# Keys, values and two retention heads move into a kernel's front, and one more conditioning job to TensorE

## What is computed

```python
c_act = silu(c)
mod = c_act @ w_ada + b_ada                 # (2048,) @ (2048, 12288)
sh1, sc1, gt1, sh2, sc2, gt2 = split(mod, 6)
h = modulate(rms_norm(x, g_mix), sh1, sc1)
proj = h @ w_in + b_in                      # 2048 x 5376
rq, rk, rv, rg, aq, ak, av = split(proj)    # 4 x 1024, 1024, 128, 128
mix = concat([retention(rq, rk, rv, rg), window_attention(aq, ak, av, sinks)]) @ w_out
x = x + gt1 * mix
h = modulate(rms_norm(x, g_ffn), sh2, sc2)
x = x + gt2 * conv_glu(h, w_up, w_conv, b_conv, w_down)    # d_ff 5632
f_shift, f_scale = split(c_act @ w_final_ada + b_final_ada, 2)
y = modulate(rms_norm(x, g_final), f_shift, f_scale)
```

## Time and profile before

| what | value |
|---|---|
| median of 3 runs | 1285.28 us (1285.04 to 1286.55) |
| the profiled execution's own time | 1290.68 us |
| its span | 1289.0 us |
| PE busy | 1215.5 us, 94% |
| DVE, ACT, POOL busy | 68%, 46%, 14% |
| DMA, mean over the span | 266 GB/s |
| mean granted clock | 0.972 |

### The profile page before, as it was taken

How to read it: one execution, slowest core, us unless ns; L and a number is a source line. 1 busy time by engine, 2 the same in 40 slices (tenths; PEclk the granted TensorE clock), 3 DMA queues, 4 the chain that set the end, 5 groups by cost and what they waited for, 6 DMA issues and landing times.

```text
span 1289.0 us, 22449 instructions
## 1 busy us (share of the span) xinstructions
PE 1215.5 (94%) x8031; PEld 1080.1 (84%) x8031; DVE 875.1 (68%) x1058; ACT 590.5 (46%) x849; POOL 174.7 (14%) x303
## 2 busy tenths in 40 slices
PE   5777799999999998999999999999999999999995
PEld 1545689897888786999999999999999987887884
DVE  1222478789698897566776767767655575778886
ACT  3221345426335345654454544545445454555442
POOL 6433111021121111000100100100000001010000
PEclk9778899999999998999999999999999999999998
DMA  9887998688699896468778787777655556887851
GB/s 358 323 309 283 350 331 287 236 301 318 239 349 348 308 336 232 163 218 287 263 276 275 265 287 264 277 273 266 209 176 182 185 189 245 286 290 253 328 214 65
DMA packets 117220, 343.03 MB, mean 266 GB/s; under 512 B 9806, under 2 KB 12336, under 8 KB 116528
## 3 DMA queue, kind: packets, MB, share of 16 engines
q1 hardware_dynamic: 79232, 206.19, 46.0%
q0 software_dynamic: 37504, 134.30, 28.6%
q10 hardware_dynamic: 432, 1.84, 0.4%
HBM read 340.20 MB, written 2.10 MB: 266 GB/s over the span
## 4 chain that ended last, share of the span: by engine, by line
PE 81%; DMA 7%; DVE 5%; issue 3%; ACT 2%; POOL 1%; POOLq 0%; ACTq 0%; DVEq 0%
PE ps L1167 26%; PE ps L1169 25%; PE ps L1168 25%; DMA arena<-in_w_ada 3%; DMA ada_raw<-in_w_ada 2%; DVE acc L767 2%; DMA raw<-in_w_in 1%; DVE wlo L757 1%; PE ps L1224 1%; PE ps L1213 1%; PE ps L1296 1%; DMA acc<-in_b_ada 1%; PE ps L1308 0%; DVE xb L1019 0%; DVE arena L1017 0%
## 5 line engine op out<-in xcount | busy, mean ns | idle before, releaser
L1167 PE MATMUL ps<-hhi,whi 128*128 128x256 f32 x1824 | 525.3, 288 | 27.0 <-DVE wlo L757 24.0
L1168 PE MATMUL ps<-hlo,whi 128*128 128x256 f32 x1824 | 520.3, 285 | 0.0
L1169 PE MATMUL ps<-hhi,wlo 128*128 128x256 f32 x1824 | 520.2, 285 | 0.0
L484 ACT ACTIVATE whi<-raw 128x1024 fp32r<-128x1024 f32 x248 | 262.7, 1059 | 346.7 <-PE ps L1169 345.2
L762 DVE TENSOR_TENSOR wlo<-raw,whi 128x1024 fp32r<-128x1024 f32 x248 | 303.3, 1223 | 134.2 <-ACT whi L484 132.3
L1167 PEld LDWEIGHTS ps<-hhi,whi 128*128 128x128 f32 x1824 | 355.5, 195 | 40.7 <-issue 35.8
L1168 PEld LDWEIGHTS ps<-hlo,whi 128*128 128x128 f32 x1824 | 355.6, 195 | 0.0
L1169 PEld LDWEIGHTS ps<-hhi,wlo 128*128 128x128 f32 x1824 | 355.2, 195 | 0.0
L767 DVE SCALAR_TENSOR_TENSOR acc<-ada_raw,c_act,acc 128x1024 f32<-128x1024 f32 (+1 forms) x192 | 245.9, 1281 | 10.4 <-DMA ada_raw<-in_w_ada 5.0
L1167 PE MATMUL ps<-whi,hhi 128*128 128x512 f32 x608 | 242.0, 398 | 3.2 <-DVE wlo L757 2.0
L1169 PE MATMUL ps<-whi,hlo 128*128 128x512 f32 x608 | 237.6, 391 | 0.0
(11 more groups left out here) (135 smaller groups left out, 615.7 us busy)
## 6 DMA issues: line engine op xcount, KB each, us to landing
raw<-in_w_up SPq DMA_DIRECT2D x176, 512.0 KB, 4.4
ada_raw<-in_w_ada POOLq DMA_DIRECT2D x160, 512.0 KB, 6.3
raw<-in_w_down SPq DMA_DIRECT2D x44, 1024.0 KB, 6.4
raw<-in_w_in SPq DMA_DIRECT2D x40, 1024.0 KB, 7.3
ada_raw<-in_w_final_ada POOLq DMA_DIRECT2D x64, 512.0 KB, 5.7
arena<-in_w_ada POOLq DMA_DIRECT2D x32, 512.0 KB, 9.1
raw<-in_w_out SPq DMA_DIRECT2D x16, 1024.0 KB, 7.5
xb<-in_x SPq DMA_DIRECT2D x2, 1024.0 KB, 6.1
```

What stands on the lines that cost most here:

```text
L484: nc.scalar.activation(whi[:, i % RING, :], raw_of(step0 + i), ACT.Copy).then_inc(hi_ready, 1)
L1167: nc.tensor.matmul(out_ap, lhs[0], rhs[0], start=start, stop=False, skip_group_check=skip)
L1168: nc.tensor.matmul(out_ap, lhs[0], rhs[1], start=False, stop=False, skip_group_check=skip)
L1169: return nc.tensor.matmul(out_ap, lhs[1], rhs[0], start=False, stop=True, skip_group_check=skip)
```

## The change

A turn of the front now has 7 steps (`FRONT`): four of attention queries, two of the retention's query heads 0 and 1 (512 columns of two 128-row tiles each) and one of keys and values. The other two heads follow as 8 steps behind the front, so 88 steps are left there. SP loads each step by itself, step i of turn `job` when unit 8 + i of that job has landed. On PE the key/value step of a turn is done in the next turn, directly behind `sum_columns`; pairs stand singly behind the first four steps of a turn, four pairs together behind the fourth query step, and the second head step comes last. DVE does the splits of three steps of the coming turn ahead of `pe_rows`. Job 4 (`JOB_SH2`) goes through PE as eight pairs behind steps p 2, 5, 9, 13, 17, 21, 25 and 29, from the same ring of four slots as DVE's units (`MIXED`). Attention: four scores a step at p 2 to 5 and 22 to 25, transposes at 12 to 19 and 31 to 34 (two heads a step), values at 14 to 21 and 33 to 36; the normalisation moves from DVE to ACT; all eight heads' transposed probabilities have room of their own (`pT = probs[:, :, 0:320]`) where two had.

The diff, cut:

```diff
-AQ_STEPS = [k if k < 12 else k + 3 for k in range(KT)]
-AK_STEPS = [12, 13, 14, 19]
+FRONT = 7
+AQ_STEPS = [FRONT * (k // 4) + (0, 1, 3, 4)[k % 4] for k in range(KT)]
+RQA_STEPS = [FRONT * (r // 2) + (2, 5)[r % 2] for r in range(KT // 2)]
+AK_STEPS = [FRONT * n + 6 for n in range(4)]
+STEP_RQB = 4 * FRONT
+HEAD_BANK = (5, 6, 7, 4)
+JOB_DVE = JOB_SH2 + 1
+MIXED = [(JOB_DVE + n // KT, n % KT, False) if i < 4 else (JOB_SH2, 2 * g + i - 4, True)
+         for g in range(KT // 2) for i, n in enumerate([4 * g, 4 * g + 1, 4 * g + 2, 4 * g + 3, 0, 0])]
+PAIR_AT = (2, 5, 9, 13, 17, 21, 25, 29)
+AQ_BANK, AK_BANK, ADA_BANK = (0, 1, 2, 4), 3, 3
...
+            for step in range(STEP_RQB):
+                job, i = divmod(step, FRONT)
+                sp.wait_ge(ada_in[i], 16 * (2 * job + 2))
+                if step == 4:
+                    sp.wait_ge(xt_ps, 8)
...
+            def mixed_units():
+                for u, (job, k, _) in enumerate(MIXED):
+                    if u < RING:
+                        pool.wait_ge(ada_pe, PAIRS * JOB_SH2 - RING + u // 2 + 1)
                     else:
+                        slot_free(u - RING)
+                    load_unit(job, k, u % RING)
...
+            hi_group(0, 0, 3)
             for job in range(4):
                 act.wait_ge(mod_ready, job + 1)
                 for k in range(4 * job, 4 * job + 4):
                     modulate(k, 0, xT[:, k, :], 0, 0)
+                hi_group(FRONT * job, 3, FRONT + 3 if job < 3 else FRONT)
...
+            def normalise(batch, part):
+                act.wait_ge(den_ready, batch + 1)
+                for i in range(4 * part, 4 * part + 4):
+                    pt = (p0, p1)[i % 2][:, i // 2, :]
+                    nc.scalar.activation(pt, pt, ACT.Copy, scale=smx[:, 5, i:i + 1]).then_inc(p_norm, 1)
...
+            for step in range(3):
+                lo(step)
             for job in range(4):
+                pe_rows(job)
                 mod_cols(job, 7, 8 * job)
+                for k in range(4 * job, 4 * job + 4):
+                    h_lo(k, 0)
+                for i in range(3, FRONT + 3 if job < 3 else FRONT):
+                    lo(FRONT * job + i)
+                    if job == 3 and i > 3:
+                        unit(i - 4)
...
+            none_at = (3, 4, 5, 6, 42, 43, 44, 57, 58, 61, 62, 70, 71)
+            two_at = (46, 48)
+            units = 3
...
             for job in range(4):
+                sum_columns(job, 7, 8 * job)
                 if job:
+                    keys_values(job - 1)
+                k = 4 * job
+                att_queries(k)
+                if job < 3:
+                    ada_pair(job + 1, 0)
+                att_queries(k + 1)
+                if job < 3:
+                    ada_pair(job + 1, 1)
+                two_heads(RQA_STEPS[2 * job], k, (0, 1))
+                if job < 3:
+                    ada_pair(job + 1, 2)
+                att_queries(k + 2)
+                if job < 3:
+                    ada_pair(job + 1, 3)
+                att_queries(k + 3)
+                if job < 3:
+                    for n in range(4, 8):
+                        ada_pair(job + 1, n)
+                two_heads(RQA_STEPS[2 * job + 1], k + 2, (0, 1))
             keys_values(3)
...
+                if p in PAIR_AT:
+                    ada_pair(JOB_SH2, PAIR_AT.index(p))
```

More of the change, by code:

```diff
@@ L599, in mix_hi @@
                                      ACT.Copy).then_inc(hhi_ready, 1)
[L603 to L604 removed]
+            for p in range(STEP_WO0 - STEP_RQB):
+                hi(STEP_RQB + p)
                 if p == 1:
@@ L794, in mod_cols @@
                 parts = mod_parts(job)
-                for kind, k, count, cols in parts:
+                for n, (kind, k, count, cols) in enumerate(parts):
                     src = ps[:, bank, col0:col0 + 8][:, cols]
@@ L1223, in ada_pair @@
                         row = 32 * (2 * j + b)
-                        last = nc.tensor.matmul(ps[row:row + 32, 5 + job % 2, :], c_pad[:, k, :],
+                        last = nc.tensor.matmul(ps[row:row + 32, bank, :], c_pad[:, k, :],
                                                 ada_of_slot(slot)[:, b * 512:(b + 1) * 512],
@@ L1284, in _, with two_heads @@
-            keys_values(3)
             def split_dims(m):
                 return slice((m // 2) * RD + m % 2, (m // 2 + 1) * RD, 2)
+            def two_heads(step, k0, heads, free=None):
+                pe.wait_ge(lo_ready, step + 1)
+                slot = step % RING
+                for h in heads:
+                    if free and h == heads[-1]:
+                        pe.wait_ge(*free)
+                    for kk in range(2):
+                        for e in range(2):
+                            first = kk * (GW // 2) + (h - heads[0]) * RD
+                            c = slice(first + e, first + RD, 2)
+                            last = passes(ps[:, HEAD_BANK[h], e * S:(e + 1) * S], (whi[:, slot, c], wlo[:, slot, c]),
+                                          (hhi[:, k0 + kk, :], hlo[:, k0 + kk, :]), k0 + kk + e == 0, True)
+                last.then_inc(step_done, 1)
@@ new lines, in att_queries @@
+            def att_queries(k):
+                pe.wait_ge(hlo_ready, k + 1)
+                pe.wait_ge(lo_ready, AQ_STEPS[k] + 1)
+                columns(AQ_STEPS[k] % RING, k, k == 0, lambda b: ps[:, AQ_BANK[b], :])
+            pe.wait_ge(cols_ready, 4)
+            for job in range(4):
+                sum_columns(job, 7, 8 * job)
+                if job:
+                    keys_values(job - 1)
[17 more added lines that the diff above has]
+                two_heads(RQA_STEPS[2 * job + 1], k + 2, (0, 1))
```

462 lines of the change are left out of this document (235 added, 227 removed).

## The result

| what | before | after |
|---|---|---|
| median | 1285.19 us (1285.04 to 1286.55, 4 runs) | 1296.68 us (1293.68 to 1299.53, 4 runs) |
| ratio |  | 1.0087 [1.0061, 1.0112] |
| profiled execution, span | 1290.68 us, 1289.0 us | 1299.53 us, 1297.8 us |
| end of the front (20 steps before, 28 after) | 169.3 us | 196.0 us |
| front's end to the start of the up projection | 340.7 us | 321.7 us |

The change made the kernel slower by 11.5 us in the median. The last three rows cut the two spans at the same places of the work: the front took **+26.7 us** for the eight steps that it took in, the stretch behind it gave back **-19.0**, and the rest is even (+1.1), in sum the 8.8 us between the spans.

What follows compares the result with a forecast made beforehand. PE (94% busy) was taken as the bound, the front limited by arriving conditioning weights and a serial chain. +8.1 - 23.0 + 7.4 - 0.4 - 2.6 + 4.3 = -6.2 us, from 1285.28 to 1279.0; range 1268 to 1291.

Steps and rivals of the forecast that it cites:

- the staircase of the front: Front turns: PE frees slots every 3.8 us, units and steps load; 36.7 us a turn, front +8.1 us, ending at 177.4.
- turn 0's addition: DVE addition ending job 0 in the front: to start at 38.5 us, from bytes loaded, against 38.06 before.
- the last unit lands at a+20: Front turn: units 10 to 15 and 4.5 steps load in 14.1 us, the last landing 20 us after the first freed slot.
- a+17: Front turn: PE alone would reach the last pairs 17 us after the first freed slot, so it waits some 3 us.
- 1.7 us a turn: Front, behind PE's 3.25 us idle gap for the addition: loss from the lowered clock, 1.7 us.
- Rival 3: Longer front turns: head step at low clock (+2.2), last units 1 us later; 39.9 us a turn, 1288.7 us; chance 0.14.
- -14.3: Stretch behind the front: steps moved out -23.0, job 4's pairs +7.4, column sums -0.4, waits gone -2.6, new waits +4.3.
- the waits for pairs: Behind steps 9, 13 and 29, PE waits for units in the four-slot ring: 0.5, 1.2 and 0.9 us.
- rival 2: Middle pairs wait for their own rows behind steps 9, 13, 17, 29: 11.5 us plus clock 5.1; 1291.4 us; chance 0.14.
- nothing: Attention staged anew: scores, transposes and values are the same matmuls at other steps, so no change in PE time.
- +7.4: Job 4's eight pairs on PE behind the front, 0.93 us each, with no idle time there to hide them.
- alone is worth nothing: DVE loses 16 rows of 1.28 us and gains one addition of 0.69; no gain, since PE does not wait for DVE.

Runs made afterwards that it cites:

- e4: Changed kernel with all seven w_in loads of a turn issued only once the job's last unit has landed; 1316.57 us, 1.024 of the kernel before.
- e2: Changed kernel with pairs 0 to 3 of the next job together directly behind the turn's key/value step; 1274.82 us, 0.9933 of the kernel before.
- e1: Changed kernel with splits ahead of a turn's addition two instead of three steps deep; 1277.15 us, 0.9927 of the kernel before.
- e6: Changed kernel with small matmuls of zeros filling PE's waits at the turns' last pairs and head step; 1286.82 us, 1.0002 of the kernel before.
- e7: Kernel before, with attention scores reordered so that a step's two come from two heads in different row halves; 1282.4 us, ratio 0.9969.
- e5: e3_both with job 4's eight pairs cut to 64 of 512 columns per matmul, loads and waits kept; 1267.42 us, 0.9852 of the kernel before.
- e3_both: Changed kernel with both edits, e1 (splits two deep) and e2 (pairs 0 to 3 early); 1267.16 us, 0.9853 of the kernel before.
- e9: e3_both with job 4 back on DVE, the ring for DVE alone and DVE's rows spread anew; 1263.69 us, 0.9813 of the kernel before.
- e11: e9 with DVE's conditioning rows moved away from steps where PE's scores wait for DVE's maxima; 1255.23 us, 0.9752 of the kernel before.

## Why the prediction was wrong

**The step that failed is the staircase of the front.** In its own terms:

| term | forecast | after |
|---|---|---|
| turn 0's addition | 38.5 us | 41.44 us |
| from a, the end of the first pair, to the end of the last pair | 21 each | 24.3, 25.0, 25.5 |
| head step behind it | 2.87 each | 3.1, 5.0, 5.0 |
| from there to the next a | 12.8 | 12.4, 13.8 |
| last turn, from there to the end of the front | 28.9 | 30.2 |
| end of the front | 177.4 | 196.0 |

The 18.6 us between the ends are 12.0 of "the last unit lands at a+20", 4.5 of head steps at the low clock, and 2.1 of the rest. I let units 10 to 15 and 4.5 steps flow at 390 GB/s from a+5.9 on, in 14.1 us. The DMA did not run at that rate: its slices from 54 to 67.5 us have 288, 361 and 354 GB/s, and from 66 to 76 us the steps took 1.68 of the 3.98 MB. Without steps beside them the pairs end at a+19.1 (e4), not at a+24.3 to a+25.5. PE's own pace was 1.2 us of the miss in a turn: a+17 and one pair is 17.9, but a single pair adds 1.19 to a step and not 0.93 (the first pairs start 4.06 apart). Over the 19.1 there are 3.2 to 3.5 us of counted waits for units, close to the 3 that I had. Another 2 to 3 us come from units taken one by one, 1.05 us for one where a pair takes 1.06, and in turns 1 and 2 from the low clock. I took the share to be harmless because the sum of bytes was right. The stops were missed in the same way: at 132 to 136 us the DMA has nothing to do, as the pairs that free slots stand behind 6 us of steps. e2 moves just those pairs, and the turns are 4 to 10 us shorter. With e1 the addition comes out from behind the split, and both together bring 30 us by the fourth addition (138.08 for 168.14). Turn 0's addition was a term that I never asked for a queue: it stood at 38.5 by bytes, but on DVE it is behind the split of step 2, whose weights come late, and it came at 41.4. The first pair ended at 51.5 all the same, 0.3 behind the forecast, because the first matmul followed the addition in 4.7 us and not in 6.9: two errors that cancelled.

**The clock.** The prediction gave it 1.7 us a turn behind the gap and kept the head step at full speed. e6 prices the clock of these ends of turns at about 10 us. In two turns of three the profile shows it low ahead of the gap already, where PE does half pairs with waits of 1.5 to 1.9 us between; turn 0 had waits of 1.6 and kept its clock to the end of the head step, so these waits do not always cost it. Rival 3 named this place and its mechanism (a head step at the low clock, turns of 39.9 us) and its 39.9 is the length of the first turn, but by luck, since that turn kept its clock. It took one more microsecond for the late units where 3.4 to 4.5 came, and so ended at 187 and 1288.7, not at 196 and above.

**Behind the front** the sum came out on the better side: -19.0 for -14.3. The moved steps, -23.0, and the waits for pairs (3.1 for the forecast 2.6) stand; rival 2, waits of 11.5, did not happen. Two gains were not in the sum: the scores run together, 4 to 5 us by e7 where I wrote "nothing", and the wait for a split at 445 us went with its loss of clock, 2.0 and 1.7. With these two it should have been about -22.5, 3.5 more than came. Of these, 0.9 are a new wait for softmax, and some 2 would be the eight single pairs at 1.19 us for 0.93, if they cost there what they cost in the front.

**Job 4 on PE.** +7.4 was a little low as the price of its matmuls (9.5 at 1.19 us each), and the wrong reading: I wrote that PE is the limit there, and e5 shows that cutting them to an eighth gives nothing, in e3_both's order. That DVE's relief "alone is worth nothing" did not hold for every order: with the 16 rows back on DVE (e9) PE waited 5.8 us for its softmax, and with the rows placed otherwise (e11) it did not. The run without the move is 3.5 us better than e3_both, and 12 with DVE's rows placed for it. How much of those last 8 is the placing and how much could have been had with job 4 on PE too was not tried.

So the change has a good part and a bad one. With the order of e3_both the same work needs 20 us less than the kernel before. The order of a turn as it was written, with the addition behind a split that needs a late load, and pairs behind the steps that they should make room for, cost all of that and 11 us more.

## What to carry to other kernels

Where two queues share the DMA, a sum of bytes over a turn gives its least time, not its time: follow the last transfer that someone waits for, and the instruction that frees the next slot, each through the queue of its engine. Put first in each engine's order what frees slots and what ends a serial chain; here that changed the sign, from +0.9% to -1.5%, with the same work. Before moving work to a busier engine, cut it there to a fraction: if nothing is gained, something else is the limit there, such as a buffer.

## What had not been expected of the hardware

PE can be "busy" for 4.00 of 4.00 us and yet have fallen to 0.50: in the changed kernel this followed half pairs with waits of 1.5 to 1.9 us between them, in two turns of three, and with filled gaps (e6) the clock stayed at 1.00 through the same stretch. And matmuls of 64 rows overlap when neighbours use different halves of the rows: in the kernel after, a batch of four scores starts at 205.55 and the next step at 206.41, 0.86 us later. Three of the kernel before, where neighbours mostly use the same half, start at 270.67 with the next step at 271.53, also 0.86.

```profile
205.55 0.93 PE L1386 MATMUL ps<-arena 64*128 64x128 f32 x8
```
